# Re-spacing the marks that pace two streams of row gathers in a fused hybrid-layer kernel

## The reference, cut to what matters

```
h  = rms_norm(x, norm1_w);  proj = h @ w_in                    # projection
x  = x + concat(stick_breaking_attention, gated_delta_net) @ w_out
# expert half, hn = rms_norm(x), 8 heads, 16 experts of 16384 per head and token
q  = hn @ w_q;  s1, s2 = scores with 128 + 128 sub-keys
best, experts = top 16 of the combined top 16 x top 16         # per token and head
act = gelu(sum_d u_table[experts] * hn) * softmax(best)
y  = x + sum_k act[k] * v_table[experts[k]]
```

## Time and profile before

| | us |
|---|---|
| median of 3 runs (3548.87 to 3561.72) | 3555.86 |
| the profiled execution's own time | 3561.24 |
| its span, first to last instruction | 3559.5 |

### The profile page before, as it was taken

The page is one execution under the profiler, slowest core; times in us unless marked ns, Lnnn a source line. Parts: engine busy times, 40 slices in busy tenths (PEclk is TensorE's granted clock), DMA queues, the critical chain, the costliest instruction groups (busy, mean ns, idle before and its releaser), DMA issues.

```text
span 3559.5 us, 46354 instructions
## 1 busy us (share of the span) xinstructions
PE 2354.7 (66%) x16193; PEld 1425.5 (40%) x16193; DVE 2318.2 (65%) x5421; ACT 849.8 (24%) x2344; POOL 2308.0 (65%) x2091
## 2 busy tenths in 40 slices
PE   7663546885847759767848859758847784344477
PEld 6543424653524436534524536534514451000011
DVE  3436887776697597666698587667696658444400
ACT  3330012331213223313114123314103311111122
POOL 1001775555667777677777677577687768777775
PEclk9887657897868879878869879878858885555555
DMA  7542899998989999999999999999999999999999
GB/s 233 190 169 97 312 356 328 351 374 301 349 321 357 410 373 411 412 381 390 409 374 387 409 384 410 368 389 395 406 371 369 407 409 346 387 409 409 409 403 374
DMA packets 398905, 1276.24 MB, mean 359 GB/s; under 512 B 44302, under 2 KB 99667, under 8 KB 389459
## 3 DMA queue, kind: packets, MB, share of 16 engines
q0 software_dynamic: 294912, 1073.87, 78.2%
q1 hardware_dynamic: 85330, 157.45, 12.2%
q10 hardware_dynamic: 18432, 41.95, 3.2%
HBM read 1232.18 MB, written 40.93 MB: 358 GB/s over the span
## 4 chain that ended last, share of the span: by engine, by line
POOL 25%; PE 24%; DVE 18%; DMA 17%; issue 9%; ACT 3%; DVEq 3%; ACTq 1%; SPq 0%; POOLq 0%
PE zz L1489 14%; POOL u_ring L684 13%; POOL v_ring L699 11%; DMA v_ring<-in_peer_v,idxT 9%; DVE u_ring L1067 5%; PE va L1489 4%; PE rr L1489 4%; DMA u_ring<-in_peer_u,idx 4%; DMA u_ring<-in_peer_v,idxT 2%; PE ox L1489 1%; DMA work<-d_w 1%; POOL u_ring L699 1%; DVE work L1398 1%; DVE work L1400 1%; DMA work<-d_gv 1%
## 5 line engine op out<-in xcount | busy, mean ns | idle before, releaser
L684 POOL DMA_INDIRECT u_ring<-in_peer_u,idx x1024 | 1177.2, 1150 | 786.4 <-DVE work L1414 330.3
L1067 DVE SCALAR_TENSOR_TENSOR u_ring<-u_ring,hn_t 128x1024 f32<-128x1024 f32 x1024 | 1223.1, 1222 | 387.2 <-DMA u_ring<-in_peer_u,idx 383.6
L699 POOL DMA_INDIRECT v_ring<-in_peer_v,idxT x960 | 1061.5, 1106 | 422.2 <-issue 248.6
L1489 PE MATMUL va<-v_ring,column 128*32 128x256 f32 x7680 | 748.3, 493 | 618.3 <-DMA v_ring<-in_peer_v,idxT 562.8
L1489 PE MATMUL zz<-work 128*128 128x256 f32 (+3 forms) x3232 | 739.0, 390 | 62.4 <-DVE work L1248 12.6
L1489 PEld LDWEIGHTS zz<-work 128*128 128x128 f32 (+1 forms) x3232 | 552.6, 212 | 270.7 <-issue 136.6
L1489 PEld LDWEIGHTS va<-v_ring,column 128*32 128x32 f32 x7680 | 196.9, 124 | 1096.9 <-DMA v_ring<-in_peer_v,idxT 888.0
L763 ACT ACTIVATE column<-onehot,wT 128x32 f32<-128x32 f32 x1024 | 285.9, 315 | 805.7 <-PE va L1489 777.5
L1489 PE MATMUL zz<-work,w_q_t 128*128 128x128 f32 x1024 | 132.0, 292 | 1.8 <-DVE work L1314 1.8
L1489 PEld LDWEIGHTS zz<-work,w_q_t 128*128 128x128 f32 x1024 | 127.1, 206 | 14.2 <-issue 11.5
L1489 PE MATMUL rr<-work,later 128*128 128x512 f32 x144 | 97.3, 796 | 40.0 <-DVE work L1267 31.1
(11 more groups left out here) (245 smaller groups left out, 2519.1 us busy)
## 6 DMA issues: line engine op xcount, KB each, us to landing
work<-d_w SPq DMA_DIRECT2D x42, 1024.0 KB, 8.5
work<-in_w_out ACTq DMA_DIRECT2D x64, 512.0 KB, 9.5
u_ring<-in_peer_u,idx POOLq DMA_INDIRECT x1024
v_ring<-in_peer_v,idxT POOLq DMA_INDIRECT x960, 10.4
work<-d_kT SPq DMA_DIRECT2D x36, 256.0 KB, 8.2
work<-d_v SPq DMA_DIRECT2D x36, 256.0 KB, 6.6
work<-in_x SPq DMA_DIRECT2D x16, 512.0 KB, 7.6
w_q_t<-in_peer_w_q SPq DMA_DIRECT2D x1, 8192.0 KB, 26.6
```

The source lines that it names most:

```text
L684: g.indirect_dma_start(u_ring[:, n % RU, :], None, u_rows, bass.IndirectOffsetOnAxis(idx[b % 2][:, s:s + 1], 0)).then_inc(u_landed[n % RU] ...
L699: g.indirect_dma_start(v_row(n), None, v_rows, bass.IndirectOffsetOnAxis(idxT[b % 3][:, t:t + 1], 0)).then_inc(v_landed[slot] if slot < RV ...
L1067: v.scalar_tensor_tensor(u_ring[:, m % RU, :], u_ring[:, m % RU, :], 1.0, hn_t[b % 2][:, :], ALU.mult, ALU.mult, accum_out=dots[:, s:s + 1 ...
L1489: return t_.matmul(out_, lhsT, rhs, start=start, stop=stop, skip_group_check=True)
```

## The change

Only the list of marks is changed. The number of rows, every instruction's form, rings, and the waits stay; what moves is how many dot products and V rows stand at which place, and the order of the gathers in POOL's list.

```
-MARKS = [(1, 0.62, 128, 0), (1, 1.0, 128, 40), (2, 1.0, 250, 118), (4, 1.0, 500, 368), (6, 1.0, 756, 624), (7, 1.0, 884, 750)]
+MARKS = [(1, 0.55, 128, 0), (1, 1.0, 128, 60), (2, 0.7, 256, 118), (2, 1.0, 256, 160), (3, 1.0, 364, 240), (4, 1.0, 503, 371),
+         (6, 1.0, 758, 628), (7, 1.0, 886, 752)]
```

## The result

The changed kernel is slower: median 3571.3 us of 8 runs (3559.2 to 3583.9) against 3555.3 of 8 before, ratio 1.0046 with a 95% interval of 1.0025 to 1.0066. I had forecast 3553 and no difference that can be measured. The time lies inside the range; the slowdown is clear of the noise, where I had forecast none. Two executions of variants further down, one of 4620.7 us and one of 3847.8, stand apart from the others of their kernel and are left out of the ratios.

What follows compares the result with a forecast made beforehand. DMA time was taken as the bound, with gains or losses only through idle DMA time. Terms 3 + 30 (block 2) + 25 - 53 + 0 - 8 (behind block 4) = -3 us gave a median of about 3553 us, range 3526 to 3576.

Steps and rivals of the forecast that it cites:

- (b): Block 2's projection: 131 rows at its places where 87 were, DMA becomes the limit, +39 us.
- (e): Block 3: 197 rows issued for 174, less half of the idle DMA time, +25 us.
- (f): Block 4: 275 rows issued for 327, taken as -53 us between bounds of -41 and -67.
- (g): Pause at V 256 in block 4 replaces that at 512 ahead of block 6: +6 and -6 us, sum 0.
- My slower rival: Block 4 does not give the rows back; at -30 us there the sum is +20, 3576 us; chance 0.22.
- (c): Block 2, start to output projection: about 9 dot products, 5 V rows and block 1's gelu more, +11 us.
- (d): Block 2 behind the output projection: no dot products where 30 stood, -18 us, nearer block 0's 75 us without rows.
- (a): Block 1: 14 more dot products before the output projection, 14 fewer behind; +22 us, -17 us, taken as +3 us.

Runs made afterwards that it cites:

- the pair at 0.70 and 0.78: The fast variant with block 2's U rows ending at 0.70 and at 0.78 of its places for 0.85: ratios 1.0051 and 0.9988 against before.
- the fast variant: Against before: the late marks, block 2's U rows ending at 0.85 of its places and V at 150, block 3 at 364 and 228; ratios 0.9911 and 0.9904.
- the late marks: The kernel before with only the changed kernel's marks of blocks 4, 6 and 7: median 3540.8 us, ratio 0.9973 against before.

## Why the prediction was wrong

**What held.** DMA time is the bound, and the change wins or loses by idle DMA time. The projection (b), block 3 (e) and block 4 (f) came within 3 us of their terms, (f) without the +6 that (g) put into block 4. In the projection POOL's wait for VectorE fell from 58.8 to 29.9 us and the share rose to 1.00, as forecast. My slower rival, that block 4 wouldn't give its rows back, was not it: it gave 55 us, on the forecast's 53. That rival had the right sign for the wrong reason, and that its 3576 kept the measured time inside the range is luck. Nor did gathers get dearer: those of U in block 1's first part took 1307 ns for 1303.

**The step that failed is (c) with (d).** I priced the places behind the projection by their dots and by VectorE's chain, +11 and -18, and wrote of the rings running dry only to count the rows issued by block 2's end. Measured: +20 and -9, together +11 for the forecast's -7: these 18 us are the largest miss of the sum. Two things stand in its place. First, the list: once U stands at its cap, POOL has nothing but V rows to issue, and a ring of eight is soon full while TensorE is in a chain. The mark at 0.70 put that moment ahead of the mixing chain, where TensorE passes no place for 20 us. Moved behind the output projection, the middle stretch falls by 24 us with as many gathers. Second, block 0's 75 us from line 1312 to 1414 is not the time of VectorE's work without dots: VectorE is busy for 52 us of it and waits 17.3 us for the scores, which TensorE's steps of pq hold back, and dot products that stand in such a wait cost nothing. In block 2 this wait rose from 5.4 to 27.7 us.

How (c) divides between POOL's stop, the gelu and turn that stood in the same stages, and the slower rows ahead of them, no run separates: moving the end of U moves all three. That POOL stands for 20.3 us without a gather is shown, and so is, by the pair at 0.70 and 0.78 with one number between them, that block 2 loses 16 us with as many gathers when U ends behind the output projection, and the kernel 0.6%. Of the changed kernel itself this leaves 1.0024 with U's end moved (on a slower chip): block 1's marks, the pause or both may hold the rest.

**Block 1 (a)** was +10 for +3. POOL's limit in the first part was read rightly (+21 for the +22); the return was 11 us for 17, by the same error as in (d): DVE's wait for the scores rose from 14.3 to 22.8 us. Before's profile is the shortest of its kind: over all profiles on the faster chips block 1 takes 300 to 306 us with the old marks and 309 or 310 with the new, which is nearer +7. As its cost in time, +0.56% alone and 0.2 to 0.6% by its removal (medians, ratios) were measured, on slower chips only.

**The pause (g)** was priced from one case as +6 and -6. Taking away the old one gave 11 us, together with four rows fewer behind block 7 and a shorter block 7; taking away the new one gave 0.6 to 0.8% on one slower chip and nothing measurable on the other, and on the faster ones 10 us of blocks 3 and 4. The old one stood in the last, light places of the projection, the new one in its middle. By these numbers the two cancel roughly in the first result, as forecast, at about twice the price.

**The chance** of 0.22 for slower was too low because I took the terms of the block where idle time is consumed and didn't ask where the next idle time opens.

The version that beats both kernels is the fast variant, 0.9 and 1.0% below before in its two runs, both on faster chips; a third of it is the late marks' gain. On the slower ones it wasn't run, and what its neighbours gained there is 0.1% at most.

## What to carry to other kernels

When two streams share one issuing queue in order, look for the moment when one of them has no work that can be issued (here: indices that don't exist yet). From there the other's ring alone feeds the DMA engines; such a moment belongs behind a chain in which its consumer passes by often, not ahead of one in which it is away for longer than the ring lasts. Work that stands in another engine's waiting time is free where it is: read what the engine will wait for when the work is gone before counting its removal as a gain. And measure on more than one chip before a change of half a per cent is called one thing or the other.

## What the runs showed of the hardware

The same program is 6.6 to 7.4% slower on some chips. The tail behind block 7, where the DMA share is 1.01 on the faster ones, moves 355 to 362 GB/s there for 394 to 397. Blocks 0 and 1 take the same time on both (the two profiles of before: 341 and 304 us for 339 and 300), every later block is longer (block 2 438 for 411, block 7 399 for 372, the tail 611 for 554), and the same marks rank a little differently. Why those chips move less is not shown.

An indirect gather holds POOL for 0.93 to 0.94 us at the least, for up to 1.99 us in the rows above and 2.35 in the whole trace of before: those of 989 and 991 us, 1.94 and 1.99, were issued while VectorE ran dot products (985.7 to 993.8 us), the one of 1013.75, 0.94, while it ran nothing. The Trainium skill, "GPSIMD Engine Reference", section 1, says that the two engines contend for SBUF when a VectorE instruction has two SBUF inputs; the direction agrees, though other gathers amid dots took 0.93 us too (the one at 985.40), and no run isolates it.
